# Two PEER expert layers on one core: the change from the up-projection to the down-projection is reordered on three engines

## The reference, cut to what matters

```python
def block(args):
    xb, ib, gb = args
    ub = jnp.take(u, ib, axis=0)
    a = jax.nn.gelu(jnp.einsum('td,ted->te', xb, ub), approximate=False)
    vb = jnp.take(v, ib, axis=0)
    return jnp.einsum('te,ted->td', a * gb, vb)
```

## Time and profile before

| what | value |
|---|---|
| runs | 2352.88, 2359.7 and 3766.18 us, median 2359.7 |
| the profiled execution's own time | 2358.1 us |
| its span in the trace | 2356.3 us |
| mean granted TensorE clock | 0.975 of full |
| TensorE matmul busy | 2255.5 us, 96% of the span |
| VectorE, ScalarE, GpSimd busy | 1487.4, 1136.2, 947.5 us |
| HBM read, written | 391.90 and 44.63 MB |

### The profile page before, as it was taken

One profiled execution on the slowest core, in us unless ns is written; L12 is line 12 of the kernel. 1 busy time (PEld: TensorE's weight loads), 2 busy tenths in 40 slices (PEclk: granted clock), 3 DMA queues, 4 the chain that ended last, 5 costly groups with the idle time before them and its releaser, 6 DMA issues.

```text
span 2356.3 us, 45223 instructions
## 1 busy us (share of the span) xinstructions
PE 2255.5 (96%) x14420; PEld 1963.8 (83%) x14420; DVE 1487.4 (63%) x3175; ACT 1136.2 (48%) x2241; POOL 947.5 (40%) x786
## 2 busy tenths in 40 slices
PE   7989999899999999999999888899999999999997
PEld 6955456799999999788787677899999998887876
DVE  5215454419938999666765734199379996667656
ACT  6523333246664444455555532556644444555554
POOL 5711111168987666001100240779876671011000
PEclk9999999999999999999999989999999999999999
DMA  4588877545554444457665532445544444575652
GB/s 164 167 233 327 350 306 283 186 144 164 185 186 144 142 142 140 148 194 265 215 217 176 180 130 79 163 144 186 179 159 139 140 141 155 183 261 192 243 176 101
DMA packets 110091, 437.69 MB, mean 186 GB/s; under 512 B 12605, under 2 KB 13205, under 8 KB 100537
## 3 DMA queue, kind: packets, MB, share of 16 engines
q1 hardware_dynamic: 92712, 335.26, 42.6%
q0 software_dynamic: 17008, 100.25, 11.8%
q10 hardware_dynamic: 288, 1.08, 0.1%
HBM read 391.90 MB, written 44.63 MB: 185 GB/s over the span
## 4 chain that ended last, share of the span: by engine, by line
PE 89%; DVE 4%; ACT 2%; issue 2%; POOL 1%; DMA 1%; ACTq 0%; POOLq 0%; DVEq 0%; SPq 0%
PE pa L434 75%; PE pb L434 14%; POOL split L1813 1%; DMA raw<-in_units 1%; DVE big L1638 1%; ACT big L991 0%; DVE halves L1638 0%; ACT split L963 0%; ACT big L1185 0%; DVE big L1754 0%; DMA big<-in_x 0%; DVE top L1318 0%; DVE big L1744 0%; DVE big L1740 0%; ACT big L1167 0%
## 5 line engine op out<-in xcount | busy, mean ns | idle before, releaser
L963 ACT CAST split<-raw 128x512 fp32r<-128x512 f32 x1176 | 722.8, 621 | 896.9 <-PE pa L434 830.9
L434 PE MATMUL pa<-xh,split 128*128 128x256 f32 (+1 forms) x5280 | 973.0, 285 | 33.7 <-DVE xl L1330 24.0
L1813 POOL TENSOR_TENSOR split<-raw,split 128x512 fp32r<-128x512 f32 x664 | 864.8, 1313 | 282.6 <-ACT split L963 240.5
L434 PEld LDWEIGHTS pa<-xh,split 128*128 128x128 f32 x5280 | 825.2, 190 | 38.6 <-issue 22.3
L434 PE MATMUL pa<-xl,split 128*128 128x256 f32 (+1 forms) x2640 | 745.9, 283 | 0.0
L434 PE MATMUL pa<-split,wsplit 128*128 128x512 f32 x3072 | 708.9, 392 | 6.4 <-DVE wsplit L1512 6.4
L434 PEld LDWEIGHTS pa<-split,wsplit 128*128 128x128 f32 x3072 | 578.8, 189 | 134.8 <-issue 14.6
L1337 DVE TENSOR_TENSOR split<-raw,split 128x512 fp32r<-128x512 f32 x512 | 353.7, 692 | 267.5 <-ACT split L963 266.1
L434 PEld LDWEIGHTS pa<-xl,split 128*128 128x128 f32 x2640 | 502.9, 190 | 0.0
L1459 DVE TENSOR_SCALAR scb<-pa,top 128x128 f32<-128x128 f32 x512 | 168.3, 396 | 0.0
L1474 DVE TENSOR_TENSOR big<-big,top 128x256 f32 (+1 forms) x128 | 139.0, 1086 | 42.1 <-ACT top L1022 29.1
(11 more groups left out here) (283 smaller groups left out, 1566.9 us busy)
## 6 DMA issues: line engine op xcount, KB each, us to landing
raw<-in_units SPq DMA_DIRECT2D x636, 512.0 KB, 3.3
big<-in_state_in POOLq DMA_DIRECT2D x20, 1024.0 KB, 9.1
out_state_out<-big POOLq DMA_DIRECT2D x20, 1024.0 KB, 7.4
halves<-in_state_in POOLq DMA_DIRECT2D x12, 1024.0 KB, 9.7
out_state_out<-halves POOLq DMA_DIRECT2D x12, 1024.0 KB, 6.8
out_c_prompt<-big POOLq DMA_DIRECT2D x4, 1024.0 KB, 5.1
bias_rows<-scb POOLq DMA_DIRECT2D x1, 3072.0 KB, 39.6
big<-in_skeys POOLq DMA_DIRECT2D x2, 1024.0 KB, 7.4
```

The source lines that it names most:

```text
L434: return pe.matmul(out, lhs, rhs, start=start, stop=stop)
L963: nc.scalar.copy(split[:, 2 * (n % 2) + half, 0, :], ring[:, slot, half * 512:(half + 1) * 512]).then_inc(high_done, 1)
L1813: nc.gpsimd.tensor_tensor(split[:, v, 1, :], ring[:, (a + k) % RING, o], split_f[:, v, 0, :], ALU.subtract).then_inc(low_done["pool"], 1)
```

## The change

It does this in each of the two layers. ScalarE's loop over the last rows ends one round of four rows earlier, and three of the four are written out; then come the wait for the 32 sets and `w_high` of rows 0 and 1, and only then row 127 (with the rounding of V unit 1 in it). The wait for the last gated rows stands behind the rounding of V unit 2, ahead of `w_high` 2. VectorE's last step is taken apart: it waits for the rows up to 125, applies the last set, makes the low part of V unit 0 and `w_low` 0, then `take_row` 126, `w_low` 1, `take_row` 127, and the low part of V unit 1. TensorE's wait for all gelus is replaced by two inside V unit 0: all but the last ahead of half 0 (banks 0 and 2), all ahead of half 1 (banks 1 and 3).

```diff
@@ TensorE, peer(L)
             pe.wait_ge(sem("gates_applied"), n0 + SETS)
-            pe.wait_ge(evacuated, group[0])
...
             def y_unit(it, k, first=False, last=False):
                 pe.wait_ge(sem("w_low"), it * RING + (NK * L + k + 1))
                 for half in range(2):
+                    if first:
+                        pe.wait_ge(evacuated, group[0] - 1 + half)
                     pe.wait_ge(low_done["dve"], it * (2 * RING) + (low0 + 2 * k + 1 + half))
@@ ScalarE, peer(L)
-            with act.Fori(1, (NK - SPREAD_AT) // RING) as it:
+            with act.Fori(1, (NK - SPREAD_AT) // RING - 1) as it:
                 for k in range(RING):
                     u_row(it, SPREAD_AT + k)
+            for k in range(3):
+                u_row((NK - SPREAD_AT) // RING - 1, SPREAD_AT + k)
             group[0] += NK
-
-            act.wait_ge(sem("row_gated"), n_r + NK - SPREAD_AT)
-            act.wait_ge(sem("gates_applied"), SETS * (L + 1))
...
+            act.wait_ge(sem("gates_applied"), SETS * (L + 1))
             w_high(None, 0)
             w_high(None, 1)
+            u_row((NK - SPREAD_AT) // RING - 1, SPREAD_AT + 3)
             for k in range(RING):
                 high_at(U_V[L] + k + 2)
+                if k == 0:
+                    act.wait_ge(sem("row_gated"), n_r + NK - SPREAD_AT)
                 w_high(None if k < 2 else 0, k + 2)
@@ VectorE, peer(L)
             gate_step(SETS // 2 - 1, 0)
-            gate_step(SETS // 2 - 1, 1, more=False)
...
+            dve.wait_ge(sem("row_gated"), n_r + NK - SPREAD_AT - 2)
+            apply(SETS // 2 - 1, 1)
             low(U_V[L] % RING, nv, 2 * nv + 1)
             w_low(0, 0)
+            take_row(0, NK - 2, n0 + SETS)
+            w_low(0, 1)
+            take_row(0, NK - 1, n0 + SETS)
             low((U_V[L] + 1) % RING, nv + 1, 2 * (nv + 1) + 1)
-            w_low(0, 1)
             y_feed(0, XS_AT)
```

More of the change, by code:

```diff
@@ L1489, in peer, with gate_step @@
                     take_row(0, SPREAD_AT + 2 * s + k, n0 + s + 1)
[L1490 to L1494, removed]
+            def gate_step(it, s):
+                dve.wait_ge(sem("gates_spread"), it * 2 + (n0 + s))
+                one_hots(it, s + 1)
                 dve.wait_ge(sem("row_gated"), it * RING + (n_r + 2 * s))
```

## The result

The kernel after takes 2342.76 us in the median of 5 runs (2340.32 to 2345.57), the kernel before 2357.36 us in the median of the 5 runs beside it. The ratio is 0.9939, with a 95% interval of 0.9925 to 0.9954: 14.4 us less, between 10.8 and 17.7. Measured once more (`e5_after_again`) it was 0.9936 (0.9922 to 0.9949). The profiled execution took 2340.59 us; its span is 17.5 us shorter than the one of before. (The run of 3766.18 us among those of before was disturbed and counts in no ratio.)

The account below looks back on a forecast made before the run. TensorE was taken to bound the kernel. Per layer, 3.17 us of gap less 0.05 plus 2.8 us of slow clock gives 5.9, twice 11.9 us: 2358.1 to 2346 us, range 2338 to 2356.

Parts of the forecast that it names:

- The gap: Between last U and first V product, TensorE's standstill of 3.17 us per layer shrinks to about 0.05.
- The slow clock: In the 6 us behind the gap, TensorE's 14 products at half rate cost 2.8 us per layer, all regained.
- Whether the clock stays: At the start of the V stage, a standstill below half a microsecond keeps the clock; around 2.2 us either way.
- Margins: In the first V units, work is ready ahead of TensorE: gelu 127 by 0.4 us, `low` of V unit 1 by 0.7.
- Rival 1: In V unit 0's half 1 or at V unit 1, TensorE waits and the clock falls: 2354 us; chance 0.10.
- Rival 2: VectorE stays behind ScalarE, so rounding comes no earlier and TensorE still waits for `w_low` 0: 2358 us; chance 0.04.
- Rival 3: ScalarE stands for code at its loop's earlier end; a 12 us stop gives 2363 us; chance 0.03.

Follow-up runs that it names:

- e5_after_again: The kernel after, unchanged, measured once more: 2340.58 us, ratio 0.9936 to the kernel before.
- e4_low_late: The kernel after, but VectorE takes rows 126 and 127 before the low parts of V unit 0 and row 0: 2357.62 us, ratio 1.0006 to before.
- e3_w_high_late: The kernel after, but ScalarE rounds rows 0 and 1 of the V stage only behind gelu 127: 2351.74 us, ratio 0.9976 to before.
- e2_one_wait: The kernel after, but with one wait for all gelus ahead of V unit 0 instead of the wait per bank: 2350.81 us, ratio 0.9979 to before.
- e1_fill_gap: The kernel before, with 24 extra unneeded products between the last U unit and the wait for the gelus, both layers: 2347.52 us, ratio 0.9967 to before.
- e9_gelu_late: The kernel after, with two extra ScalarE copies of about 1 us each behind `w_high` 1, ahead of gelu 127: 2349.4 us, ratio 0.9968 to before.
- e8_before_again: The kernel before, unchanged, timed against itself as a null: 2356.36 us, ratio 1.0003.

## Why the prediction was right

- **Sign and size.** Forecast 2346 us, 11.9 us less; measured 2342.76, 14.4 us less, in the range. The two stretches with the change in them give 12.5 us in the trace: the first V product comes 3.3 to 3.4 us sooner behind the last gate product (forecast 3.12), and the V stage behind it is 2.8 to 3.0 us shorter (forecast 2.8).
- **The gap, 3.17 us per layer less 0.05.** Right: the chain has one piece of TensorE's work across the change of stage. `e4_low_late` and `e3_w_high_late` show that both lists had to change, and `e2_one_wait` that the wait per bank is worth 1.4 us per layer, where the working had 1.1 (952.96 to 954.1).
- **The slow clock, 2.8 us per layer.** Right as a mechanism, and as a size for the profiled execution: `e1_fill_gap` took it away alone and gained 2.9 us in each layer. It is not a constant, though: the second trace of before has 1.4 us of it in layer 0 (375.0 us from gate to last V product against 376.4), `e4_low_late` 1.5, and `e3_w_high_late` 1.6. So the 2.8 us is the upper of two sizes that were seen, and that the trace of before had it in both layers was in part luck: the change gains between 1.4 and 2.9 us per layer by this term. What decides between the two sizes no run shows.
- **Whether the clock stays.** The bound from two gaps of 2.2 us held. The series now is: 0.2 and 0.6 us, no fall; 1.2 us, no fall in two cases; 1.8 us, one fall in two; 2.2 us (the start of the U stages, the nine traces of the table), a fall in 11 of 18, which cost 1.6 to 1.7 us each; 3.0 to 3.2 us, a fall in all six.
- **Margins.** Gelu 127 was named as the tight point, with 0.4 us, and `low` of V unit 1 with 0.7 us. In the trace after the first is 0.2 us: half 0 starts at 948.36 and runs for the 1.34 us of the working, to 949.70, and gelu 127 ends at 949.46. `e9_gelu_late` makes the first bind and not the second.
- **Rivals.** Rival 1 (a later wait) did not happen, and where it was made to happen it was too short for the clock to fall. Rival 2 is out by VectorE's timeline. Rival 3 is out: ScalarE's timeline has no gap at the written-out rows that TensorE does not explain. (Its argument counted five packets of code; a second queue brought two more in that stretch.)
- **The 1.9 us between the 12.5 of the trace and the 14.4 of the timing.** The prediction has no term for it. It is within the interval (from 10.8 us), and the second measurement, 15.1 us (12.0 to 18.4), is so too, but both lie on the same side. In both traces of the kernel after the middle stage loses 13.4 us to the clock, and in the other seven of the table 15.5 to 18.0, `e1_fill_gap` with its clock at 1.00 across the change of stage among them. Its length is 0.6 us or more below theirs. Whether the time of the change of stage decides the clock of the next one, and so brings a part of the gain, stays open.

## What to carry to other kernels

A standstill of TensorE costs itself and can cost half rate behind it, here 3.2 us and then 1.4 to 2.9 us; look at the granted clock of the microseconds behind the gap, not only at the wait. Between two stages, put the next stage's preparation where the engines stand idle for the last products of this one, and make TensorE wait for each bank by itself; such an edit counts only when all the lists that feed the first product have it. Where the gap cannot be closed, products that nobody needs can hold the clock, as they did here. Do not add up the clock's price over several gaps: the one at the start of the U stage gained half of its price when it was closed, and the filled norms gave back less than a third of the work that they kept from half rate. And compare the unchanged stages of two traces before the timed difference is put down to an edit.

## What the runs showed of the hardware that was not expected

- Behind equal standstills of 3.2 us in one execution the half rate lasted about 3 us in one layer and 6 us in the other (`e8_before_again`: 51 and 45 products in the 16 us from the start of the standstill). Counted with a full-rate pace of 0.224 us a product, the half rate took away 1.4 us and 2.8 us.
- A standstill of 1.8 us was enough for the clock to fall in one layer, and was not in the other; 2.2 us did either too, a fall in 11 of 18 cases.
- Edits that cost 2.8 and 1.8 us in the stretches where they were made (`e2_one_wait`, `e9_gelu_late`) moved the median by 7 to 10 us against the kernel after; by their traces most of it lies in stages whose code was the same, as lost clock.
